# The mixing layer's long filter two microseconds ahead of its lane, and the sums of q's squares three steps later

## What is computed

```python
def mixing_layer(...):
    u = jnp.einsum("bsd,de->bse", h, w_in)
    a_b, a_c, a_x, q, k, v, c_in = jnp.split(u, offs, axis=-1)
    y_a = a_b * causal_depthwise_conv(a_c * a_x, short_conv_w)        # 3 taps
    ...
    o = diff_attention(q, k, v, lam)                                  # 4 heads
    o = rmsnorm(o, diff_subln_g) * (1.0 - lam_init)
    ...
    c = c[..., :CONF_WIDTH] * jax.nn.sigmoid(c[..., CONF_WIDTH:])
    c = causal_depthwise_conv(c, conf_dw_w) + conf_dw_b               # 31 taps
    y_c = jax.nn.silu(layernorm(c, conf_ln_g, conf_ln_b))
    y = jnp.concatenate([y_a, y_b, y_c], axis=-1)
    return jnp.einsum("bse,ed->bsd", y, w_out)

def _gated_deltanet(q, k, v, alpha, beta, a_log, dt_bias):
    q = _l2norm(q) * (A_DK ** -0.5)                                   # needs the sum of q*q over 128 channels
    k = _l2norm(k)
    ...
```

## Time and profile before

| | us |
|---|---|
| median of 3 runs (lowest, highest) | 2757.39 (2756.61, 2765.16) |
| the profiled execution | 2750.45 |
| its span | 2749.2 |
| busy in the span: PE, DVE, ACT, POOL | 2617.6 (95%), 1094.9 (40%), 950.4 (35%), 1184.0 (43%) |
| mean granted PE clock | 0.975 of full |

### The profile page before, as it was taken

One profiled execution on the slowest core, in us unless ns is written; L12 is line 12 of the kernel. 1 busy time (PEld: TensorE's weight loads), 2 busy tenths in 40 slices (PEclk: granted clock), 3 DMA queues, 4 the chain that ended last, 5 costly groups with the idle time before them and its releaser, 6 DMA issues.

```text
span 2749.2 us, 32971 instructions
## 1 busy us (share of the span) xinstructions
PE 2617.6 (95%) x12952; PEld 2126.7 (77%) x12952; DVE 1094.9 (40%) x2297; ACT 950.4 (35%) x1440; POOL 1184.0 (43%) x1573
## 2 busy tenths in 40 slices
PE   7989999999989999998999999989999999999997
PEld 5767888887758888876877787767786787888886
DVE  6874111125863111136555754332435432311112
ACT  4443322234533312235333233222544333321221
POOL 3123655641125656653232322234333564565654
PEclk9999999999989999998999999989999999999998
DMA  5531222237422223231110101013221332222222
GB/s 186 135 105 62 92 88 104 88 105 178 129 62 83 96 90 107 80 137 60 47 47 31 47 31 47 31 46 131 77 83 57 115 113 86 90 89 93 104 86 76
DMA packets 41802, 241.50 MB, mean 88 GB/s; under 512 B 4656, under 2 KB 5808, under 8 KB 18480
## 3 DMA queue, kind: packets, MB, share of 16 engines
q1 hardware_dynamic: 38768, 218.43, 22.8%
q0 software_dynamic: 2880, 20.97, 3.8%
HBM read 214.21 MB, written 4.19 MB: 79 GB/s over the span
## 4 chain that ended last, share of the span: by engine, by line
PE 84%; DVE 9%; ACT 2%; issue 2%; DMA 1%; POOL 1%; SPq 0%; DVEq 0%; ACTq 0%; POOLq 0%
PE PB L1696 66%; PE PB L1734 4%; PE PB L1698 4%; DMA WL<-WR 1%; ACT WH L1956 1%; POOL WL L2725 1%; PE PB L1880 1%; PE PB L1716 1%; PE PB L1877 1%; PE PB L1911 1%; PE PB L1892 1%; PE PB L1708 1%; PE PB L1770 1%; DVE NEWT L2232 1%; PE PB L1899 1%
## 5 line engine op out<-in xcount | busy, mean ns | idle before, releaser
L2725 POOL TENSOR_TENSOR WL<-WR,WH 128x256 fp32r<-128x256 f32 x1412 | 1011.1, 752 | 805.2 <-ACT WH L1956 805.2
L1696 PE MATMUL PB<-HH,WH 128*128 128x512 f32 x1992 | 806.4, 405 | 12.1 <-ACT HH L1971 9.0
L1696 PE MATMUL PB<-HL,WH 128*128 128x512 f32 x1992 | 785.2, 394 | 3.4 <-DVE HL L2253 3.3
L1696 PE MATMUL PB<-HH,WL 128*128 128x512 f32 x1992 | 524.6, 399 | 8.8 <-DMA WL<-WR 6.1
L1956 ACT ACTIVATE WH<-WR 128x2048 fp32r<-128x2048 f32 (+1 forms) x209 | 371.6, 1778 | 266.9 <-PE PB L1696 262.5
L1696 PEld LDWEIGHTS PB<-HH,WH 128*128 128x128 f32 x1992 | 378.8, 190 | 104.8 <-issue 15.2
L1696 PEld LDWEIGHTS PB<-HL,WH 128*128 128x128 f32 x1992 | 378.7, 190 | 86.1 <-DVE HL L2253 8.9
L1696 PEld LDWEIGHTS PB<-HH,WL 128*128 128x128 f32 x1992 | 368.7, 190 | 89.6 <-issue 8.1
L1696 PE MATMUL PB<-BH,WH 128*128 128x512 f32 x848 | 336.8, 397 | 9.1 <-ACT BH L1984 9.1
L1696 PE MATMUL PB<-BL,WH 128*128 128x512 f32 x848 | 336.0, 396 | 6.6 <-POOL BL L2737 5.8
L1696 PE MATMUL PB<-BH,WL 128*128 128x512 f32 x848 | 210.3, 394 | 0.0
(11 more groups left out here) (340 smaller groups left out, 3040.8 us busy)
## 6 DMA issues: line engine op xcount, KB each, us to landing
WR<-in_w_gu SPq DMA_DIRECT2D x66, 1024.0 KB, 4.8
WR<-in_w_dn SPq DMA_DIRECT2D x48, 704.0 KB, 4.0
WR<-in_w_in SPq DMA_DIRECT2D x22, 1024.0 KB, 4.8
WL<-WR POOLq DMA_DIRECT2D x20, 1024.0 KB, 7.0
WR<-in_qkv SPq DMA_DIRECT2D x12, 1024.0 KB, 4.8
WR<-in_w_out SPq DMA_DIRECT2D x8, 1024.0 KB, 4.7
WR<-in_qk SPq DMA_DIRECT2D x8, 1024.0 KB, 4.9
WR<-in_gb SPq DMA_DIRECT2D x4, 1024.0 KB, 4.9
```

What stands on the lines that cost most here:

```text
L1696: ins = pe.matmul(out[:, 0:n], wt[:, k * cols + j * P:k * cols + (j + 1) * P], x[:, k, 0:n], start=first, stop=last)
L2725: ins = g.tensor_tensor(m.WL[u % 2][:, part], m.WR[u % 2][:, part], f32(m.WH[u % 2][:, part]), ALU.subtract)
```

## The change

The long filter's lane gets a lead of 2.0 model microseconds: after each of its steps its time is set 2.0 earlier than before, so it is picked ahead of lanes that stand up to that far behind. And in `prepare` the column sums of q's squares are placed behind the row spread and the transposed v.

```diff
--- before.py
+++ after.py
@@ -332,6 +332,8 @@
     "mqin": [("V", 0.7, 0)], "xscore": [("T", 0.9, 0)], "xmax": [("V", 0.8, 0)], "xexp": [("A", 0.8, 0)], "xnorm": [("V", 0.7, 0)],
     "xtrans": [("T", 0.3, 0)], "xcopy": [("A", 1.3, 0)], "xpv": [("T", 1.8, 0), ("A", 0.7, 0)],
 }
+
+FILTER_LEAD = 2.0
 BY_BLOCK = ("score", "smax", "sexp", "snorm", "strans", "spv", "bscore", "bsc", "bexp", "bnorm", "btrans", "bpv")
 
 
@@ -484,7 +486,9 @@
 def weave(clock, stream, slack, *lanes):
 
 
-    live = [[clock.free["T"], i, g] for i, g in enumerate((stream,) + lanes)]
+
+    lanes = [(stream, 0.0)] + [g if isinstance(g, tuple) else (g, 0.0) for g in lanes]
+    live = [[clock.free["T"], i, g] for i, (g, _) in enumerate(lanes)]
     stuck = 0
     while live:
         it = min(live)
@@ -496,7 +500,7 @@
             stuck = 0
             continue
         if clock.steps > before:
-            it[0], stuck = clock.lane + slack if it[1] else clock.free["T"], 0
+            it[0], stuck = clock.lane + slack - lanes[it[1]][1] if it[1] else clock.free["T"], 0
         else:
             it[0] = max(it[0], min([x[0] for x in live if x is not it], default=0.0)) + 0.05
             stuck += 1
@@ -927,7 +931,7 @@
             got["fo"] = follow(f"ffn{l}", gain_of(f"ffn_g{l}"))
             yield from residual(f"w_out{l}", 4, ys, got["fo"], ks=[0, 2, 3, 6, 7, 1, 4, 5], fine=True)
 
-        weave(clock, lane(heads_in(0), heads_in(1), short_conv(), mixed()), 0.4, *lanes, conv_taps())
+        weave(clock, lane(heads_in(0), heads_in(1), short_conv(), mixed()), 0.4, *lanes, (conv_taps(), FILTER_LEAD))
         return ffn(l, got["fo"], m.ff1, then)
 
 
@@ -1036,13 +1040,13 @@
             room3, t3 = row("p8", h)
             kt_done = t3.done
             yield from fbank.left(1)
+            room2, t2 = row("prow", h, 0)
+            yield from fbank.left(1)
+            room4, t4 = row("p5", h)
+            yield from fbank.left(1)
             room = fbank.take()
             t = Tile(room, room.after)
             qq.free(pe("colsum", "q", h, tile=t, src=m.SQ[qq.i], tok=at("p1q", h), nb=4, j0=0))
-            yield from fbank.left(1)
-            room2, t2 = row("prow", h, 0)
-            yield from fbank.left(1)
-            room4, t4 = row("p5", h)
             cfree[f"v{i}"] = [t4.done]
             step("p2", h, tile=t3, q=junk.i, after=junk.after + kn_done[i])
             junk.free(at("pks", h))
```

## The result

The changed kernel takes 2732.03 us (median of 5 runs, 2726.15 to 2740.06) against 2756.64 (5 runs, 2754.23 to 2765.16): 24.6 us less, ratio 0.9905, 95% interval 0.9881 to 0.993. The forecast was 20.8 us less, 2736.5.

The account below looks back on a forecast made before the run. PE, busy 95% of the span, was taken as the bound, so only its idle or low-clock time could be won. 26.3 − 10 + 4.5 = 20.8 us saved, from 2757.4 to 2736.5 us, range 2721 to 2751.

Parts of the forecast that it names:

- The tail: End of both mixing layers: with the filter done early, the output projection reaches its second job sooner, saving 26.3 us.
- The walk: Step-by-step timing from S, the output projection's first matmul, through the norm of heads 2 and 3 to the second job.
- the term of which 1.2 was charged: End of each mixing layer: 1.2 us more for products that follow while PE's clock is still low.
- S + 18.2: Forecast start of the second job, 18.2 us after the output projection's first matmul, against 31.6 and 31.1 before.
- The middle: Middle of the mixing layers: earlier taps, waits and moved PE work cost 4 us in layer 0, 6 in layer 1.
- Table loads: Four added ACT loads of 1.28 us each, charged nothing because ACT is busy only 25.64 of 48 us there.
- prepare: Second block: later column sums let other steps run in PE's waits for ACT's squares of q, saving 4.5 us.
- The hand-over of the tail: Rival: heads 2 and 3 hold the projection for most of what the filter held; 2751 us, chance 0.09.
- the crowded DVE: Rival: PE's waits in the middle of the layers come to 10 us each, not 5; 2746.5 us, chance 0.16.
- slower: Rival: the filter's norm is exposed in the middle, up to 18 us a layer; 2767 us, chance 0.05.
- The table loads on the path: Rival: the four loads delay the second pair's exp, costing 5.1 us; 2741.7 us, chance 0.04.
- More than forecast: Rival: the clock stays up or the waits are covered, saving 34 us; 2723 us, chance 0.12.

Follow-up runs that it names:

- lead_only: The changed kernel with the column sums of q's squares back where they stood before, only the filter's lead kept: 2733.2 us against 2754.7 before.
- sums_mid: The changed kernel with the column sums of q's squares behind the row spread but ahead of the transposed v: 2728.0 us against 2754.7 before.
- pair_nolead: The changed kernel with each output projection's first two jobs side by side and the filter's lead set to 0: 2752.5 us against 2757.7 before.

## Why the prediction held

**The tail (26.3 us; by the rows 27.3).** From the projection's first matmul to the third job, layer 0 took 37.1 us (226.47 − 189.35) and takes 23.1 (216.32 − 193.18), layer 1 36.6 and 23.3: 14.0 and 13.3 saved, where 13.4 and 12.9 were forecast. The walk goes step by step: the last `BL` is done at S + 13.1 by the forecast and at S + 12.8 by DVE's rows (205.98), and after one more product the eight low ones start at S + 13.4 (206.62). They take 3.42 us at 0.43 us each, the second job begins at S + 16.9, and four of its products run at 0.43 us too before the clock is back at 211.73. Those four cost 0.8 us, the term of which 1.2 was charged, so the forecast's S + 18.2 answers to S + 17.7. The forecast read the clock of before as back at 220.98; the window from 219 to 220 us has 0.72, so it was back at about 219.6.

**The middle (10 us; by the rows 9.3).** The projection starts 3.8 us later in layer 0 (4 forecast), and in layer 1 the stretch from the first rotation to it is 5.5 us longer (134.88 against 129.38; 6 forecast). Its composition was not as told. The taps ended early enough that PE takes the sum of `cc` at 125.01 without a wait (1 us forecast) and waits only 0.77 us for its squares (2). The moved PE work is 2.7 us (1.3, 0.9 and 0.5 for the sums, the squares' sums and the spread) and not 2.2. A wait of 0.48 us at a head's transposes came on top. The old wait of 1.24 us at a v product is gone whole (1 forecast), and so is one of 0.43 at a score. That makes 2.2 us of the 3.8. The rest is no wait; part of it lies at the v products that follow another kind of matmul, where the next starts 0.5 us later instead of 0.12 (126.32 to 126.84), and the remainder stays open. So the forecast's 4 us came out right with the waits put too high and the work too low, which is luck. DVE's late read-outs in layer 1 show as forecast: 1.6 us at the rotations.

**The two together.** 27.3 − 9.3 = 18.0 against a forecast 16.3. The lead alone gives 19.0 in its trace and 21.5 by its runs (interval 19.0 to 27.0).

**Table loads (0).** Right in size: the kernel with none of them has its landmarks at the same times. But the reason given, ACT's busy share of the stretch, is not what makes them free: the one load stands ahead of a wait for data and the other behind the result that DVE waits for. Loads ahead of that result are paid, though ACT has free time over the stretch. The Trainium skill (ScalarE: Activation LUTs, What ACT_TABLE_LOAD costs) prices a switch at 2.66 us with its drain. The loads in these traces take 1.28 us and the next activation starts right behind them, so the rows show no drain. By the page's price, as an estimate, eight on the path would be 21 us; 10 to 13 were measured, with small activations among them.

**`prepare` (4.5; measured 6.2, interval 2.2 to 10.5).** The squares' waits fell from 12.1 to 3.3 us, not to 5, but 4.3 us of waits for v's `silu` took their place, so that the sum, 7.6, is 4.5 less than before, the forecast's figure. That it hits is partly luck, since the forecast put the squares at 5 and named v's `silu` without a figure for it. The stretch itself got shorter by more than its waits: 10.9 us against the first profile of before, 6.4 against the second, some 8 by the means of all profiles. Where the 3 us beyond the waits come from was not found.

**The rivals.** The hand-over of the tail is refuted: heads 2 and 3 hold the projection for no longer than the walk said. So are the crowded DVE and "slower" at a lead of 2: the filter's norm costs PE 0.77 us of wait in the middle of each layer. A lead of 8 brings about both, late scores and an exposed norm; that its 2767.1 us meet the figure of "slower" is chance. (That rival counts 94 v products beside the norm; by the orders there are 88 to 90.) The table loads on the path are refuted by the kernel without them. "More than forecast" has part of the truth: the clock's charge was too high, and the waits in the middle of layer 0 were fewer than charged.

## What to carry to other kernels

Work that ends last and needs nothing late can be issued ahead of the lanes that end with it, as long as the engine that does it has free time where it lands; with the lead it was 20 us, and with four times the lead all of it was gone and 9 us more. When such a chain is gone, look at what the stage now ends in and put the next job's ready products beside it: that was worth another 15 us, and nothing that could be told without the first step. And compare a second profile of the kernel before, before explaining a stretch that no edit touches: the kernel without the four table loads reaches the landmark on `S` at the changed kernel's time and still ends 7.0 us later.

## What the runs showed that was not expected

Two executions of one kernel differ in where the granted clock drops. The first profile of before has 1.00 from 2060 to 2190 us, and the second 0.90 and 0.96; the changed kernel and the one without the loads have 0.52 from 618 to 625 us with PE busy throughout, at products that in before, `lead_only` and `sums_mid` run at 1.00. Such stretches cost some 3 us each and can make up most of the scatter of some 7 us either way. What decides them was not found. A partly idle stretch of PE lies ahead of or in each of those looked at, but it is not enough: from 610 to 618 us PE is busy 6.13 of 8 us in the changed kernel and 6.08 in `lead_only`, and only the first drops. In the tail it is not chance: before and `pair_nolead` have 0.67 from 190 to 221 us, and with the idle time filled it is 1.00.
